# Where the normed input's rows begin: 544-word rows, compact low rows and five tiles of per-channel columns in a fused two-block kernel

## What is computed

```python
# first block (528 tokens)
hn = rmsnorm(h)
proj = hn @ w_in     # q, k, v, z, a, b of the delta rule; q, k, v of stick-breaking attention; two gates
o_dn = gated_delta_rule(...); o_sb = stick_breaking_attention(...)
h += (sigmoid(gate_dn) * (o_dn @ w_branch_dn) + sigmoid(gate_sb) * (o_sb @ w_branch_sb)) @ w_out
h += swiglu(rmsnorm(h))
# second block (512 tokens): layer 0 attention, layer 1 Hyena, each with adaLN and a convolutional FFN
```

## The kernel before

| operand | before |
|---|---|
| `spl`, `raw` | 0 |
| `HNH`, `HNL` row k, first word | 64k (0, 64, 128, 192, 0, ...) |
| the same, 265th word (second half of `x_all`) | 32 + 64k |
| the same, 17th token (`x_meta`) | 64 + 64k |
| `HSH`, `HSL` all rows | 0 |
| `VOH/L`, `OSH`, `MGH/L`, `AFH/L`, `OGH/L`, `ZH/L` all rows | 0 |
| `OSL` row k | 64k |

## Time and profile before

### The profile page before, as it was taken

One profiled execution on the slowest core, in us unless ns is written; L12 is line 12 of the kernel. 1 busy time (PEld: TensorE's weight loads), 2 busy tenths in 40 slices (PEclk: granted clock), 3 DMA queues, 4 the chain that ended last, 5 costly groups with the idle time before them and its releaser, 6 DMA issues.

```text
span 2898.9 us, 39863 instructions
## 1 busy us (share of the span) xinstructions
PE 2788.2 (96%) x15611; PEld 2259.8 (78%) x15611; DVE 1309.8 (45%) x1932; ACT 708.9 (24%) x1094; POOL 1603.8 (55%) x1569
## 2 busy tenths in 40 slices
PE   8999989999999999999999989999999998999999
PEld 8998878799678787888875568888777455788887
DVE  6677562311720575343336733331286678433311
ACT  3375223532620002010025621110111222211100
POOL 7653124655076665666651147666685534676664
PEclk9999999999999999999999999999999999999999
DMA  4211001222023565556520013333322000233321
GB/s 130 85 62 36 2 2 45 87 74 88 1 75 100 181 207 161 191 176 209 182 94 30 30 58 93 97 107 100 102 88 91 30 7 15 88 93 97 107 100 69
DMA packets 292585, 260.22 MB, mean 90 GB/s; under 512 B 6617, under 2 KB 264390, under 8 KB 292156
## 3 DMA queue, kind: packets, MB, share of 16 engines
q1 hardware_dynamic: 289492, 250.83, 26.9%
q0 software_dynamic: 2416, 6.34, 0.7%
q10 hardware_dynamic: 504, 0.66, 0.1%
HBM read 255.72 MB, written 2.10 MB: 89 GB/s over the span
## 4 chain that ended last, share of the span: by engine, by line
PE 84%; DVE 6%; issue 4%; DVEq 2%; ACT 2%; POOL 1%; DMA 1%; POOLq 0%; ACTq 0%; SPq 0%
PE ps L536 23%; PE ps L537 23%; PE ps L538 23%; PE ps L1770 1%; PE ps L1750 1%; PE ps L1613 1%; PE ps L1593 1%; PE ps L1603 1%; PE ps L1337 1%; PE ps L1735 1%; PE ps L1358 1%; PE ps L1676 1%; PE ps L939 1%; PE ps L1365 1%; PE ps L1269 1%
## 5 line engine op out<-in xcount | busy, mean ns | idle before, releaser
L825 POOL CAST spl<-raw 128x512 fp32r<-128x512 f32 (+1 forms) x352 | 247.3, 703 | 648.8 <-PE ps L538 518.7
L536 PE MATMUL ps<-HSH,spl 128*128 128x512 f32 x1344 | 536.1, 399 | 20.2 <-DVE HSL L747 16.2
L827 POOL TENSOR_TENSOR spl<-raw,spl 128x512 fp32r<-128x512 f32 (+1 forms) x352 | 496.7, 1411 | 56.6 <-issue 6.7
L537 PE MATMUL ps<-HSL,spl 128*128 128x512 f32 x1344 | 527.6, 393 | 0.0
L538 PE MATMUL ps<-HSH,spl 128*128 128x512 f32 x1344 | 527.4, 392 | 0.0
L831 POOL TENSOR_TENSOR spl<-raw,spl 128x512 fp32r<-128x512 f32 (+1 forms) x352 | 479.6, 1363 | 51.5 <-issue 1.3
L536 PE MATMUL ps<-HNH,spl 128*128 128x264 f32 (+1 forms) x1152 | 365.7, 317 | 3.4 <-DVE HNL L717 2.9
L537 PE MATMUL ps<-HNL,spl 128*128 128x264 f32 (+1 forms) x1152 | 356.7, 310 | 0.0
L538 PE MATMUL ps<-HNH,spl 128*128 128x264 f32 (+1 forms) x1152 | 355.6, 309 | 0.0
L829 POOL CAST spl<-raw 128x512 fp32r<-128x512 f32 (+1 forms) x352 | 232.0, 659 | 208.1 <-PE ps L538 206.0
L536 PEld LDWEIGHTS ps<-HSH,spl 128*128 128x128 f32 x1344 | 254.5, 189 | 95.2 <-issue 38.4
(11 more groups left out here) (459 smaller groups left out, 4404.2 us busy)
## 6 DMA issues: line engine op xcount, KB each, us to landing
adw<-in_ada_w SPq DMA_DIRECT2D x96, 512.0 KB, 5.5
raw<-in_w_in SPq DMA_DIRECT2D x44, 1024.0 KB, 5.0
raw<-in_ffn_w_up SPq DMA_DIRECT2D x88, 512.0 KB, 4.6
raw<-in_w_ffn_in SPq DMA_DIRECT2D x44, 512.0 KB, 4.7
raw<-in_ffn_w_down SPq DMA_DIRECT2D x16, 1408.0 KB, 6.0
raw<-in_hy_w_in SPq DMA_DIRECT2D x12, 1024.0 KB, 5.0
raw<-in_w_ffn_out SPq DMA_DIRECT2D x8, 1408.0 KB, 6.3
raw<-in_w_branch_dn SPq DMA_DIRECT2D x8, 1024.0 KB, 4.9
```

The lines of the kernel that those rows point to most:

```text
L536: pe.matmul(dst, w[0], x[0], start=first, stop=False)
L537: pe.matmul(dst, w[0], x[1], start=False, stop=False)
L825: pool.tensor_copy(hi[:, first, :], w[:, first, :])
L827: pool.tensor_tensor(lo[:, first, :], w[:, first, :], hi[:, first, :], ALU.subtract).then_inc(split_first, 1)
```

## The change

The normed input's rows get 544 words in place of 528 (only 528 are used), and the first row begins so that its 17th token lies on a multiple of 128 bytes. `LINE` goes from 128 words to 32. The pad ahead of `raw` goes; a 16-word `tiny` now lies between `H` and `HNH` and takes its place. `HSH`, `HSL`, `HS` and the Hyena stage's `YF` begin 16 words into the old place, at the first row's 17th token. `OSL` gets rows of 512 words. The per-channel rows are packed into five tiles, and `gsc` and `csil` move into free columns of `pcol`. No loop, queue, wait or arithmetic changes.

```diff
-        [("norm_mix", 8), ("dn_gain", 2), ...  ("skip", 16)],
-        [("hy_w", 72), ("hy_b", 24)],
-        [("ada_b", 96)],
-        [("fc_w0", 66), ("fc_b0", 22)],
-        [("fc_w1", 66), ("fc_b1", 22)],
+        [("ada_b", 96), ("hy_b", 24), ("csil", 8)],
+        [("hy_w", 72), ("fc_b0", 22), ("fc_b1", 22), ("norm_mix", 8), ("dn_gain", 2), ("sbq", 1), ("sbk", 1)],
+        [("fc_w0", 66), ("norm1", 16), ("norm2", 16), ("skip", 16), ("norm_ffn", 8)],
+        [("fc_w1", 66), ("final", 8), ("gq", 1), ... ("b2", 1), ("c", 8), ("gsc", 32)],
...
-        LINE = 128
-        tiny = fresh("tiny", 8)
-        gsc = fresh("gsc", 2, 2, KD)
-        csil = fresh("csil", KD)
-        here[0] += -(top[0] // 4 + here[0]) % LINE
+        LINE = 32
         raw_at = here[0]
         raw = fresh("raw", 2, SLOT)
         spl = fresh("spl", 2, 2, SLOT // 2, dtype=F32R)
         H = fresh("H", KD, T)
+        TW = -(-T // LINE) * LINE
+        tiny = fresh("tiny", LINE - META)
         hn_at = here[0]
-        HNH = fresh("HNH", KD, T, dtype=F32R)
+        HNH = fresh("HNH", KD, TW, dtype=F32R)[:, :, 0:T]
         lo_at = here[0]
-        HNL = fresh("HNL", KD, T, dtype=F32R)
-        HSH = at("HSH", [KD, SEQ], hn_at, dtype=F32R)
-        HSL = at("HSL", [KD, SEQ], lo_at, dtype=F32R)
+        HNL = fresh("HNL", KD, TW, dtype=F32R)[:, :, 0:T]
+        here[0] -= TW - T
+        hs_at = hn_at + META
+        assert (top[0] // 4 + hs_at) % LINE == 0
+        HSH = at("HSH", [KD, SEQ], hs_at, dtype=F32R)
+        HSL = at("HSL", [KD, SEQ], lo_at + META, dtype=F32R)
...
+        gsc = cols("gsc", 0, 4 * KD).rearrange("p (l n k) -> p l n k", l=2, n=2)
+        csil = cols("csil", 0, KD)
...
         work = here[0]
+        assert (top[0] // 4 + work) % LINE == 0
...
-        OSL = at("OSL", [2 * HEADS, T], work, dtype=F32R)
+        OSL = at("OSL", [KD, SEQ], work, dtype=F32R)
```

More of the change, by code:

```diff
@@ L48, in _rows @@
         [("conv_q", 32), ("conv_k", 32), ("conv_v", 64)],
-        [("norm_mix", 8), ("dn_gain", 2), ("sbq", 1), ("sbk", 1), ("norm_ffn", 8), ("norm1", 16),
-         ("norm2", 16), ("final", 8), ("gq", 1), ("gk", 1), ("freq", 1), ("b1", 1), ("b2", 1),
-         ("c", 8), ("skip", 16)],
-        [("hy_w", 72), ("hy_b", 24)],
-        [("ada_b", 96)],
-        [("fc_w0", 66), ("fc_b0", 22)],
-        [("fc_w1", 66), ("fc_b1", 22)],
+        [("ada_b", 96), ("hy_b", 24), ("csil", 8)],
+        [("hy_w", 72), ("fc_b0", 22), ("fc_b1", 22), ("norm_mix", 8), ("dn_gain", 2), ("sbq", 1), ("sbk", 1)],
+        [("fc_w0", 66), ("norm1", 16), ("norm2", 16), ("skip", 16), ("norm_ffn", 8)],
+        [("fc_w1", 66), ("final", 8), ("gq", 1), ("gk", 1), ("freq", 1), ("b1", 1), ("b2", 1), ("c", 8), ("gsc", 32)],
     ]
@@ L142, in sem @@
             return ctx.enter_context(nc.semaphore(name))
-        LINE = 128
-        tiny = fresh("tiny", 8)
-        eps, zero = tiny[:, 0:1], tiny[:, 1:2]
-        gsc = fresh("gsc", 2, 2, KD)
-        csil = fresh("csil", KD)
-        here[0] += -(top[0] // 4 + here[0]) % LINE
+        LINE = 32
         raw_at = here[0]
@@ L157, in build @@
         H = fresh("H", KD, T)
+        TW = -(-T // LINE) * LINE
+        tiny = fresh("tiny", LINE - META)
+        eps, zero = tiny[:, 0:1], tiny[:, 1:2]
         hn_at = here[0]
-        HNH = fresh("HNH", KD, T, dtype=F32R)
+        HNH = fresh("HNH", KD, TW, dtype=F32R)[:, :, 0:T]
         lo_at = here[0]
-        HNL = fresh("HNL", KD, T, dtype=F32R)
-        HN = at("HN", [KD, T], lo_at)
-        HSH = at("HSH", [KD, SEQ], hn_at, dtype=F32R)
-        HSL = at("HSL", [KD, SEQ], lo_at, dtype=F32R)
-        HS = at("HS", [KD, SEQ], lo_at)
+        HNL = fresh("HNL", KD, TW, dtype=F32R)[:, :, 0:T]
+        HN = at("HN", [KD, TW], lo_at)[:, :, 0:T]
+        here[0] -= TW - T
[3 more added lines that the diff above has]
+        HSL = at("HSL", [KD, SEQ], lo_at + META, dtype=F32R)
+        HS = at("HS", [KD, SEQ], lo_at + META)
         def normed(n):
@@ L357, in build @@
         ytmp = at("ytmp", [2, SEQ], norm_at)
-        here[0] = hn_at
+        here[0] = hs_at
         YF = fresh("YF", 2, 4, SEQ)
@@ L361, in build @@
         KS = fresh("KS", 4, SEQ)
-        assert here[0] <= hn_at + 2 * KD * T
+        assert here[0] <= hn_at + 2 * KD * TW - (TW - T)
         here[0] = raw_at + SLOT + 2 * NT * SEQ // 2
@@ L1518, in _ @@
             pe.wait_ge(split_x, NT + KD)
-            pe_gemm(pe, branch_sb, lambda k: (OSH[:, k, :], OSL[:, k, 0:SEQ]), after=ada_after(branch_sb))
+            pe_gemm(pe, branch_sb, lambda k: (OSH[:, k, :], OSL[:, k, :]), after=ada_after(branch_sb))
             pe_gemm(pe, mix_out, lambda k: (MGH[:, k, :], MGL[:, k, :]), lambda k: (merged, k + 1), ada_after(mix_out))
@@ L2636, in _ @@
             for k in range(KD):
-                split_tile(dve, QSK[:, k, 0:SEQ], OSH[:, k, :], OSL[:, k, 0:SEQ]).then_inc(split_x, 1)
+                split_tile(dve, QSK[:, k, 0:SEQ], OSH[:, k, :], OSL[:, k, :]).then_inc(split_x, 1)
             for t in range(KD):
```

## The result

The changed kernel takes 2926.66 us (median of 4 executions, 2923.68 to 2932.12) beside 2898.61 us (4 executions, 2896.53 to 2900.44) for the kernel before: ratio 1.0099, 95% interval 1.0087 to 1.0112. That is 28 us slower. The forecast was 2895.7, the range ended at 2914. The profiled execution took 2928.28 us.

What follows compares the result with a forecast made beforehand. TensorE was taken to bound the kernel, busy for 2788.2 of 2898.9 us. The terms -3.8 - 0.8 + 0.7 + 0 - 0.2 = -4.1 us took the median of 2899.75 to 2895.7, range 2890 to 2914.

Steps and rivals of the forecast that it cites:

- part 4: Tensors moved along (`spl`, everything from `work` on) go from 0 to 128: no cost; 12.5 us if 128 is bad.
- weights against inputs: Rival, chance 0.05: the row's start relative to `spl` counts; `HSH`/`HSL` go out of step, 19.8 us more, 2919.3 us.
- Part 1, the 17th token: `x_meta`'s 768 matmuls, rows now at multiples of 128, each gain 4.9 ns: 3.8 us less, or nothing.
- Part 2, `OSL`: 192 matmuls of the `OSL` stage go from 231.1 to 226.8 ns: 0.8 us less, or nothing.
- Part 3, the halves of 264: `x_all`'s 2688 matmuls with new half starts cost 0.25 ns more each: 0.7 us more.
- Its sign for the failure: `HSL` 128x512 mean above 390 ns would mean that the weights' place counts.
- Part 5, `pcol`: The copy of `pcol` before the first normed row shrinks from 768 to 640 columns: 0.16 us less.

Runs made afterwards that it cites:

- e3: The changed kernel with the three norm tiles ahead of the normed input in place of `tiny`, so `HSH`/`HSL` begin at 128 like the weights; 2902.12 us, ratio 1.0010.
- e4: The kernel before with five tiles and only the normed input (`HNH/HNL`, `HSH/HSL`) moved by 128 bytes, `spl` and `work` at 0; 2925.02 us, ratio 1.0082.
- e1: The kernel before with the five tiles and the weights `spl` alone 128 bytes further; 2933.93 us, ratio 1.0116.
- e12: As e11, but the row k = 3 of eight begins 64 bytes ahead of a multiple of 256; 2899.51 us, ratio 1.0011.
- e11: The kernel before with `x_meta` rows read from the next multiple of 256 bytes (wrong tokens, same work), so all begin where the weights do; 2907.24 us, ratio 1.0020.
- e10: The kernel before with everything from `raw` on moved by 64 bytes, weights and inputs alike; 2898.82 us, ratio 1.0001.
- e8: The kernel before with `OSL` rows of 512 words and weights of k-tile k 64(k+1) bytes further in dn_z, gate_dn, gate_sb; 2899.05 us, ratio 0.9998.
- e6: As e1, but `spl` 64 bytes further; 2948.18 us, ratio 1.0167.
- e7: As e1, but `spl` 32 bytes further; 2947.65 us, ratio 1.0165.

## Why the prediction was wrong

**The step that failed** is in part 4: "`HSH`/`HSL` stay at 0, so their 3 x 1344 matmuls keep their pace as far as it hangs on them alone." It doesn't hang on them alone. The change dropped the pad ahead of `raw`, which moved `spl` to 128, and left `HSH`/`HSL` at 0. Their 4032 matmuls went from 226.8 ns to 232.5 and 233.4, and their stages took 23.7 us more. e3 and e4 show both directions: with the pair in step again 24.5 us come back, and with the pair alone out of step the kernel before loses 26.6 us. The half sentence "as far as" became the rival *weights against inputs*, and that is what happened. It was given 0.05, since "nothing in the rows asks for it". That was true but weak: all weights of the kernel before lie at 0, so its rows separate no start of a row from a difference of starts. A rival that the trace can't see should have had a larger share, and the end of the range with it.

**The rival's price** was 2919.3; measured 2926.66. A matmul out of step all the time costs 5.7 to 6.6 ns more (232.5 and 233.4 beside 226.8), not the 4.9 of gate_dn, where every fourth row was in step. That alone would be 23 us or more over 4032. Yet where the stages can be compared at like clock they are 5.2 (first FFN), 3.0 (Hyena's input) and 6.1 us (last FFN) longer in e1, and 5.8 us (attention's FFN) in e4. That is 20 us, since in qkv and in the Hyena's input TensorE often waits for others. So the 19.8 us were near by luck: a cost that was too low, times matmuls that don't all set the time. The other 7 us or so, as an estimate from one profile of each kernel, are about 1 us for the 233.4 ns in the attention's FFN and otherwise the granted clock, in the attention (3.3), in the FFN behind it and in the Hyena's input. No step of the prediction had them.

**Part 1, the 17th token** (-3.8): +0.1 over the three stages. The rows lie at 0 and 128 by turns against weights at 128, so half are out of step, and e12 shows that each such row also slows those behind it. Had it worked as meant, e11 has it at 1.8 + 0.9 + 0.1 = 2.8 us, with one wait for GpSimd in gate_dn. "GpSimd can give way" was too simple for that stage, where it was busy for 36.6 of 39 us before.

**Part 2, `OSL`** (-0.8): -1.0 at the same clock, right in size, with luck in the reason. Rows at 128 gain because the weights lie there too; the place of the weights was no part of the condition.

**Part 3, the halves of 264** (+0.7): right in size. Stages of `x_all` are 0.8 + 0.2 = 1.0 us longer; the second, with a granted clock of 1.00 in both kernels, is the cleaner one, 0.2 ns for each of its 1152 matmuls where the forecast had 0.25. The mean of the `HNL` group fell by 2 ns while the stages grew: a mean of durations isn't the pace, as the prediction said itself.

**Part 4, the work region** (0): right, for the wrong reason. Rows at 128 are fast because the weights are there too. With the weights alone at 128 (e1) they are slow, and counting 128-byte pieces of a row explains nothing: at 64 for both (e10) the pace is full.

**Its sign for the failure** was set wrong. "`HSL` at more than 390" held before the change already: the group's mean was 393, since it includes first matmuls and the lower clock. What tells is 398 beside 393, or the pace.

**Part 5, `pcol`** (-0.16): the copy took 0.80 us, 0.78 predicted. VectorE at the start, start us and us:

```profile
18.70 0.80 DVE L2323 COPY pcol<-ps 128x640 f32<-128x640 f32 x1
19.55 0.77 DVE L721 SCALAR_TENSOR_TENSOR HN<-H,pcol,ps 128x528 f32<-128x528 f32 x1
```

Of the gain next to nothing is left at the first normed row in this profile: the copy began 0.11 us later and the row 0.01 us sooner (19.55 beside 19.56).

**Two rules weighed.** By the Trainium skill, "SBUF — State Buffer", Who interferes with whom, TensorE reads moving rows and weights through two independent ports. By that rule e1 would be free; it cost 35 us. By the same page's Specifications (TRN2), SBUF has cachelines of 16 bytes, and by that rule all these starts would be equal. The trace disagrees with both as far as pace goes.

**What stays open.** That the two reads of TensorE, the row's and the next weights', meet somewhere is argued from e1 and e8, not shown: no run timed one without the other. Why a constant difference of 128 bytes runs at 232.5 ns in one stage and at 233.4 in another is open. So is why the granted clock falls in some executions. Being out of step isn't enough: e4 kept 1.00 in the attention, and e11 and e12, with more rows in step than the kernel before, lost it there.

## What to carry to other kernels

Where operands of one matmul are laid out by hand, look at all of them together: it was the remainder of row and weights by 256 bytes relative to each other that counted, so a pad that looks idle may be what holds 4032 matmuls in step. Before a tensor is moved for its own alignment, list what is moved along with it and what stays, and read every pair against each other. And where the trace shows one value of a quantity only (all weights at 0), an argument from it can't exclude that quantity: give that case a chance by the number of instructions behind it.

## What the runs showed of the hardware

- A 128x512 float32r matmul starts every 226.8 ns when moving row and weights begin at the same remainder by 256 bytes (both at 0, at 64 or at 128), and every 232.4 to 233.4 ns when the remainders differ by 32, 64 or 128 bytes (last FFN's input: 232.5 at 128 in e1, 233.4 at 64 in e6 and at 32 in e7). The absolute start didn't count.
- The slower pace outlasts its cause: a single row out of step (three matmuls, e12) cost 38 ns, and single matmuls were longer up to five behind it (393 beside 389 ns).
- `HNL` 128x264 stayed at 283 to 286 ns in every layout tried.
- Executions of one kernel differed by up to 16 us with the mean granted clock: the kernel before took 2894.62 us at 0.984 and 2910.61 at 0.978, e12 2897.31 at 0.982 and 2910.44 at 0.977.
